# A fourth seven-product block in each trip of the down projection, at slab 0 of the first trip and slab 2 of the second

## What is computed

```python
h = rmsnorm(x, norm_ffn_g[l])
x = x + jnp.square(jax.nn.relu(h @ w_up[l])) @ w_down[l]
return rmsnorm(x, final_g)
```

## Time and profile before

| what | value |
|---|---|
| time, median of 3 runs | 1507.49 us (1506.97 to 1507.68) |
| the profiled execution's own time | 1507.86 us |
| its span, first to last instruction | 1506.1 us |
| busy share PE / DVE / ACT | 99% / 83% / 52% |
| mean granted TensorE clock | 0.999 |

### The profile page before, as it was taken

One profiled execution on the slowest core, in us unless ns is written; L12 is line 12 of the kernel. 1 busy time (PEld: TensorE's weight loads), 2 busy tenths in 40 slices (PEclk: granted clock), 3 DMA queues, 4 the chain that ended last, 5 costly groups with the idle time before them and its releaser, 6 DMA issues.

```text
span 1506.1 us, 21236 instructions
## 1 busy us (share of the span) xinstructions
PE 1493.8 (99%) x7618; PEld 1263.8 (84%) x7618; DVE 1248.7 (83%) x1669; ACT 778.6 (52%) x974; POOL 2.0 (0%) x11
## 2 busy tenths in 40 slices
PE   8999999999999999999999999999999999999998
PEld 7888888888888888888888888888888888888886
DVE  6668889988889879988976779987898779987897
ACT  5544444465554456556565455545554545544554
POOL 0000000000000000000000000000000000000000
PEclk9999999999999999999999999999999999999999
DMA  9666665655556666665655656655666566656662
GB/s 301 192 182 191 189 195 179 211 180 178 176 179 197 192 198 196 209 205 188 196 182 180 194 183 210 209 186 177 209 197 207 169 202 205 195 179 209 210 203 89
DMA packets 209980, 291.12 MB, mean 193 GB/s; under 512 B 9227, under 2 KB 129107, under 8 KB 209778
## 3 DMA queue, kind: packets, MB, share of 16 engines
q1 hardware_dynamic: 209906, 290.14, 61.1%
HBM read 287.48 MB, written 2.10 MB: 192 GB/s over the span
## 4 chain that ended last, share of the span: by engine, by line
PE 99%; DMA 0%; ACT 0%; SPq 0%; DVE 0%; issue 0%
PE acc L1491 27%; PE acc L1510 14%; PE acc L1511 14%; PE acc L1512 14%; PE acc L1489 13%; PE acc L1561 3%; PE acc L1560 3%; PE acc L1559 3%; PE acc L1484 2%; PE acc L1587 1%; PE acc L1486 1%; DMA y_tok<-in_x 0%; PE acc L1639 0%; PE acc L1660 0%; PE acc L1529 0%; PE acc L1531 0%
## 5 line engine op out<-in xcount | busy, mean ns | idle before, releaser
L579 ACT ACTIVATE w_hi<-w_raw 128x1024 fp32r<-128x1024 f32 x502 | 524.4, 1057 | 441.5 <-PE acc L1512 237.5
L846 DVE TENSOR_TENSOR w_lo<-w_raw,w_hi 128x1024 fp32r<-128x1024 f32 x502 | 605.4, 1221 | 139.8 <-ACT w_hi L579 135.8
L1491 PE MATMUL acc<-h_hl,w_hi 128*128 128x512 f32 x1740 | 546.7, 395 | 0.0
L1489 PEld LDWEIGHTS acc<-h_hl,w_lo 128*128 128x128 f32 x1740 | 322.3, 188 | 72.4 <-issue 0.6
L1489 PE MATMUL acc<-h_hl,w_lo 128*128 128x256 f32 x1740 | 343.6, 279 | 0.0
L1491 PEld LDWEIGHTS acc<-h_hl,w_hi 128*128 128x128 f32 x1740 | 265.2, 189 | 0.0
L1510 PE MATMUL acc<-w_hi,m_hl 128*128 128x512 f32 x424 | 165.3, 390 | 0.0
L1512 PE MATMUL acc<-w_hi,m_hl 128*128 128x512 f32 x424 | 165.0, 389 | 0.0
L1511 PE MATMUL acc<-w_lo,m_hl 128*128 128x512 f32 x424 | 165.0, 389 | 0.0
L1510 PE MATMUL acc<-w_hi,h_hl 128*128 128x512 f32 x336 | 132.2, 394 | 0.0
L1512 PE MATMUL acc<-w_hi,h_hl 128*128 128x512 f32 x336 | 130.8, 389 | 0.0
(11 more groups left out here) (270 smaller groups left out, 1654.7 us busy)
## 6 DMA issues: line engine op xcount, KB each, us to landing
w_raw<-in_w_in SPq DMA_DIRECT2D x200, 512.0 KB, 4.4
w_raw<-in_w_up SPq DMA_DIRECT2D x128, 512.0 KB, 4.3
w_raw<-in_w_down SPq DMA_DIRECT2D x128, 512.0 KB, 4.5
w_raw<-in_w_mix_out SPq DMA_DIRECT2D x32, 512.0 KB, 4.0
w_raw<-in_w_sconv_out SPq DMA_DIRECT2D x16, 512.0 KB, 3.8
w_raw<-in_w_attn_out SPq DMA_DIRECT2D x16, 512.0 KB, 4.3
w_raw<-in_w_conf_out SPq DMA_DIRECT2D x16, 512.0 KB, 3.8
bias_row<-in_gate_b SPq DMA_DIRECT2D x10, 256.0 KB, 4.3
```

Of the source, the lines that this page charges most:

```text
L579: act.activation(w_hi[:, q], w_raw[:, raw], ACT.Copy).then_inc(hi_done, 1)
L846: dve.tensor_tensor(w_lo[:, q], w_raw[:, raw], w_hi[:, q].bitcast(F32), ALU.subtract).then_inc(lo_done, 1)
L1489: pe.matmul(*narrow[m], start=False, stop=False)
L1491: last = pe.matmul(*wide[m], start=False, stop=final)
```

## The change

Two new orders of the first four slabs of a down trip, a new step in `quads`, and a function `quad_at` that finds a block in the following trip, so that its weight sums can be prepared in the trip before. The last up trip of a chunk leaves its loop and is written out, because it now prepares the block at step 0 of the down trip behind it. The last down trip of all keeps its one block. That makes 7 blocks more: 4 at step 0 (first down trip of each chunk), 3 at step 2 (second down trip of chunks 0 to 2).

```diff
+EARLY = [(0, 1), (1, 1), (0, 0), (1, 0)]
+LATE = [(0, 0), (1, 0), (0, 1), (1, 1)]
...
+    if ph.name == "down" and t == 0:
+        return [(n, i, KDOWN) for n, i in EARLY + PAIR[4:] + PAIR_ENDS[False]]
+    if ph.name == "down" and not last_trip(ph, c, t):
+        return [(n, i, KDOWN) for n, i in LATE + PAIR[4:] + PAIR_ENDS[False]]
...
-    return (6,) if last_trip(ph, c, t) else (6, 10, 14)
+    if t == 0:
+        return (0, 6, 10, 14)
+    return (6,) if last_trip(ph, c, t) else (2, 6, 10, 14)
+
+
+def quad_at(ph, c, t, k):
+
+    if k >= ph.nslabs and ph.name == "up" and isinstance(t, int) and t == ph.trips - 1:
+        ph, t, k = PH["down"], 0, k - ph.nslabs
+    if k >= ph.nslabs and ph.name == "down" and t == 0:
+        t, k = 1, k - ph.nslabs
+    return (ph, c, t, k) if k in quads(ph, c, t) else None
...
-        loop("up", c, first=1)
+        loop("up", c, first=1, last=1)
+        body(PH["up"], c, PH["up"].trips - 1)
...
-                if k + 2 in quads(ph, c, t):
-                    act.wait_ge(t_raw, quad_of(ph, c, t, k + 2) * 2 + 2)
+                if quad_at(ph, c, t, k + 2):
+                    act.wait_ge(t_raw, quad_of(*quad_at(ph, c, t, k + 2)) * 2 + 2)
...
-                    if k + 3 in quads(ph, c, t):
-                        forms_second(ph, c, t, k + 3)
+                    if quad_at(ph, c, t, k + 3):
+                        forms_second(*quad_at(ph, c, t, k + 3))
                     if k == 15 and paired(ph, c, t) and ph.name != "A":
                         corner_sums(ph, c, t)
                     lo(ph, c, t, k)
                     if k == 0 and trip_behind(ph, c, t):
                         token_sums(*trip_behind(ph, c, t))
-                    if k + 4 in quads(ph, c, t):
-                        forms_first(ph, c, t, k + 4)
-                    if k + 2 in quads(ph, c, t):
-                        forms_lo(ph, c, t, k + 2, 0)
-                    if k + 1 in quads(ph, c, t):
-                        forms_lo(ph, c, t, k + 1, 1)
+                    if quad_at(ph, c, t, k + 4):
+                        forms_first(*quad_at(ph, c, t, k + 4))
+                    if quad_at(ph, c, t, k + 2):
+                        forms_lo(*quad_at(ph, c, t, k + 2), 0)
+                    if quad_at(ph, c, t, k + 1):
+                        forms_lo(*quad_at(ph, c, t, k + 1), 1)
...
+                if k == 0:
+                    pe.wait_ge(lo_done, s + 2)
+                    pe.wait_ge(t_lo, quad * 2 + 2)
+                    pe.wait_ge(f_lo, c * 4 + (stored + 1 + AHEAD_FORMS))
+                    pe.wait_ge(p_sum, pair_of(ph, c, t) * P_SUMS)
+                    product(P_BANK["P6"], form(S2), summed(T2), True, False)
+                    product(P_BANK["P7"], form(S3), summed(T3), True, False)
+                    product(P_BANK["P5"], form(S1), summed(T1), True, False)
+                    product(P_BANK["P1"], whole(0, 2 * i), loaded(w_x, 0), True, False)
+                    pe.wait_ge(evac_done, group_of(ph, c, t, 0) - 1)
+                    product(4, whole(0, 2 * i + 1), loaded(w_x, 1), True, False).then_inc(slab_used, 1)
+                    product(5, whole(1, 2 * i + 1), summed(T4), True, False)
+                    pe.wait_ge(evac_done, group_of(ph, c, t, 1) - 1)
+                    product(6, form(S4), loaded(w_y, 1), True, False).then_inc(slab_used, 1)
+                    return
                 pe.wait_ge(lo_done, s + 1)
                 product(4, whole(0, 2 * i + 1), loaded(w_x, 1), False, closing)
                 pe.wait_ge(t_lo, quad * 2 + 1)
```

More of the change, by code:

```diff
@@ L148, in quad_of @@
         return t * 3 + at
-    return GATE_QUADS + at if ph.name == "mix" else c * (3 * PH["down"].trips) + t * 3 + (at + GATE_QUADS + MIX_QUADS)
+    return GATE_QUADS + at if ph.name == "mix" else c * 8 + t * 4 + (at + GATE_QUADS + MIX_QUADS)
 def pair_of(ph, c, t):
@@ L167, in trip_behind @@
         return ph, c, t - 1
-    if ph.name == "up" and isinstance(t, int) and not (isinstance(c, int) and c == 0):
+    if ph.name == "up" and isinstance(t, int) and t == 0 and not (isinstance(c, int) and c == 0):
         return PH["down"], c - 1, PH["down"].trips - 1
@@ L201, in walk, with loop @@
 def walk(eng, body):
-    def loop(name, c=0, first=0):
-        with eng.Fori(first, PH[name].trips) as t:
+    def loop(name, c=0, first=0, last=0):
+        with eng.Fori(first, PH[name].trips - last) as t:
             body(PH[name], c, t)
@@ L575, in hi @@
                 q = ahead % RING
-                if ahead - 1 in quads(ph, c, t):
+                if quad_at(ph, c, t, ahead - 1):
                     act.activation(half_rows(w_hi[:, q], 1), half_rows(w_raw[:, raw], 1), ACT.Copy).then_inc(hi_done, 1)
@@ L841, in lo @@
                 dve.wait_ge(hi_done, s + (LOOKAHEAD + 1))
-                if k + LOOKAHEAD - 1 in quads(ph, c, t):
+                if quad_at(ph, c, t, k + LOOKAHEAD - 1):
                     dve.tensor_tensor(half_rows(w_lo[:, q], 1), half_rows(w_raw[:, raw], 1),
@@ L1508, in products_as @@
                         final = (n, i, a, m) == (1, KDOWN - 2, DKT - 1, 1)
+                    if 0 in quads(ph, c, t):
+                        first = first and (n, m) == (1, 1)
                     h_h, h_l = (act_hl[:, kt, h, m * P:(m + 1) * P] for h in range(2))
```

## The result

The changed kernel took 1535.84 us (median of 4 runs, 1533.99 to 1536.67) against 1507.35 us before: a ratio of 1.0186, 95% interval 1.0174 to 1.0199. It is slower by 28.5 us, where 20.6 were forecast (1528.1, range 1514 to 1540). So the time lies inside that wide range, but outside the forecast's own range of 1525 to 1532. The profiled execution took 1536.34 us with a span of 1534.6.

The account below looks back on a forecast made before the run. PE's matmul stream was taken as the bound: waits of 11.3 and 14.1 us less a 4.76 us gain make 20.6 us more, 1528.1 us. Own range 1525 to 1532; 8-in-10 range 1514 to 1540.

Parts of the forecast that it names:

- What bounds the kernel: Whole kernel: PE's matmul stream, busy 99%, sets the time; removed matmuls gain in full, waits lose in full.
- the gain of 4.8 us: Seven new blocks each save 3 matmuls, 0.68 us; 4.76 us in all if nothing waits.
- Place one: Start of each chunk's first down trip: PE waits for DVE's weight sums, 2.82 us in 4 chunks, 11.3 us.
- Place two: Start of second down trip: 1.75 us before corner sums, 2.94 us inside the step 2 block; 3 chunks, 14.1 us.
- The 0.2 us from DVE's end to PE's start: At each new wait: PE's first full-size matmul starts 0.2 us after the DVE operation that releases it.
- The other edits: Written-out up trip: four more borders cost 0 to 1.2 us, from sequencer losses of 2.0 us in 8 places; taken as 0.
- The clock: Forecast: full clock. Rival: half clock costs 2.72 us at each of 7 places (1547) or 10 waits (1555); 9%.
- DVE's delay running on: Rival: the 0.6 and 1.5 us margins behind the waits break, up to 1.5 us more in 3 or 4 chunks, 1532 to 1540; 6%.
- one place only: Rival: just part of the waits at the two down-trip starts occurs; 1514, 1516.8 or 1519 us; 9%.
- hidden work: Rival: extra DVE work hides at all new blocks, so the whole gain stands, 1502.7 us; 7%.
- exact balance: Rival: the waits at the new blocks just cancel the gain, within 0.2%; 3%.
- The DRAIN you can't avoid: Documented rule: every DVE operation waits for the pipe to empty; independent ones 0.1 us dearer, sum some 6 us higher, 1534.

Follow-up runs that it names:

- e6: e5 with the loop over chunks 1 and 2 written out as straight code; 1504.49 us, ratio 0.9980 to the kernel before.
- e2: The changed kernel without the three blocks at step 2, keeping those at step 0; 1520.61 us, ratio 1.0088.
- e4: The changed kernel with the step 0 block's products reordered, each waiting only for what it reads; 1526.57 us, ratio 1.0123.
- e3: The changed kernel without the four blocks at step 0, on the loops of the kernel before; 1524.00 us, ratio 1.0108.
- e8: The changed kernel with corner sums ahead of second weight sums, and first low part ahead of token sums, in DVE's queue; 1532.18 us, ratio 1.0167.
- e1: The kernel before with only the last up trip of a chunk written out, no new block; 1512.82 us against 1507.58.
- e5: The changed kernel without step 2 blocks, with e4's waits and step 0's weight sums two steps earlier in the last up trip; 1509.77 us.
- e7: The kernel before with the loop over chunks 1 and 2 written out, nothing else; 1507.41 us against 1507.49.

## Why the prediction was right, and where it fell short

*What bounds the kernel.* Right: every wait of PE went into the time in full (the books above come out within 0.1 us), and the gain of 4.8 us as well; e6 shows it without waits, 2.9 us for four blocks.

*Place one.* Right in place, releaser and size: 2.82 us forecast for each chunk, about 2.8 measured; the DVE chain ran within 0.1 us of the one written down from paces. The slack of 1.5 us behind it held. e2 shows it by itself, and e4 shows that the block's first wait is the cause: with the waits apart it goes.

*Place two.* Right: 1.75 and 2.94 us forecast, 1.53 + 0.28 and 2.55 + 0.28 measured in chunk 0. e3 shows both waits by themselves, and e8 that another order of the same operations in the last steps takes away only 0.6 of the 4.6 us. An earlier start of the sums was not tried there.

*The 0.2 us from DVE's end to PE's start.* Right at place one (0.21), too much inside the block at step 2 (0.05). With the release varied and the borders added the sum gives 1529.3 to 1529.6 at most, not the 1529.8 that the prediction names; nothing hangs on it.

*The other edits.* This is the step that failed: "I take 0" for the trip written out. It was bounded from 0 to 1.2 us by PE's waits at borders of trips. Alone it costs 5.2 us (e1), some 3.2 of it waiting and the rest a clock that then falls, and in the changed kernel 3.1 us of waiting. The eight places of that row are weight loads between 312 and 448 us, in code ahead of the MLP that is written out, and PE's matmuls didn't wait there. The jump that matters is the one back over the whole chunk, which cost nothing before; no row of the trace of before showed its price, and the bound from above was taken from another kind of place. e1, e3 and e5 to e7 tie it to that jump and to the longer body together: neither costs anything without the other.

*The clock.* The forecast took it at full speed, and the rival took it to fall at 7 or at 10 places for 2.72 us each. It fell at 3 of the places in the profiled run, for 1.7 us each, 5.0 us: between the two. The prediction named a clock that sinks in the down trips as a sign that it would be wrong, and in this part it was. The reasoning that 1.75 us of idleness at 10.15 us had not lowered it was no bound for waits of 2.5 us. The Trainium skill's page TensorE: Matmul & The Clock Gate, section "HAM oscillation", was the warning, and it was weighed too low: e3 shows the fall at every one of its three pairs of waits, though PE works for over 160 us between the pairs. Nor did the page's picture come true, a fall at every wait: here it was 3 of 10.

*DVE's delay running on, one place only, hidden work, exact balance.* None of them happened. The weighing of the Trainium skill's "The DRAIN you can't avoid" (VectorE: DVE Perf Modes) against the rows came out for the rows: DVE's operations without a wait between them started 1.13 to 1.14 us apart again (891.89 - 890.75). The prediction read that section too strictly: it also says that a next operation that is not held starts earlier.

The miss of 7.7 us is so the jump's 3.1 and the clock's 5.0, less 0.3 by which the waits were taken too high. The range went up to 1540 to take in a DVE delay that runs on. That didn't happen, and two terms taken at nothing filled the same room: that the time still lies in the range is luck, while the 25 us of waits and the gain of 4.8 are not.

## What to carry to other kernels

An engine at 83% may have no room at a given place: add its operations to the last few microseconds before the deadline, at their paces from start to start, from the last time at which another engine sets its clock. Before adding a seven-product block, look for where its preparation can stand earlier, and let each product wait for its own inputs alone. A loop written out partly is an edit of its own: time it alone, and look in the view of transfers whether the second pass through a loop fetches instructions again.

## What the runs showed of the hardware

- At a jump back over a loop body that had grown by one written-out trip PE stood idle for 1.9 to 3.1 us in two waits (e1: 0.83 and 2.31; the changed kernel: 1.46 and 1.34; e5: 1.01 and 1.66; e2: 0.90 and 1.54; e4: 0.90 and 1.07; e8: 0.85 and 1.08), most of them put down to issue, with 58 transfers of instructions instead of 46. The shorter body had cost nothing, and its second pass fetched no instruction in 190 us. From which length on it is fetched again was not tried.
- Waits of 2.5 to 2.6 us of a PE that is otherwise without gaps were enough for the granted clock to fall to 1.2 GHz, but not each time: in the profiled run of the changed kernel at 3 of the 7 of this length, and at none of the three of 1.4 to 1.5 us; in e3 at all three pairs; in e2 at 1 of 4; in e8 at none of seven. At the jump it fell in e1 and e5, for nearly 7 us, and not in e2, e4, e8 and the changed kernel. A fall behind a block's wait cost 1.7 us. What decides between two waits of the same length was not settled.
- The same program scattered by up to 5 us where such waits stood (e1: 1510.74 to 1513.73, with the mean granted clock going from 0.999 to 0.996; e4: 1522.92 to 1528.07; but e3 by 0.9 us), and by 0.6 us where there were none (e6).
